# A two-layer decoder trunk on one core: input and memory rows loaded already turned, query and key heads turned by VectorE

## The reference

```
proj = rms_norm(x, a_norm) @ a_w_in      # q, k (4 heads of 96), v, o (4 heads of 192), gates (8), mq (256)
hm   = mlstm_chunkwise(q, k * 96**-0.5, v, i, f)       # f32
mo   = memory_attention(mq, *memory_kv(mem))            # 4 heads of 64 over 256 memory rows
x    = x + concat(rms_norm(hm) * sigmoid(o), mo) @ a_w_out
```

## Time and profile before

| | us |
|---|---|
| median of 3 runs (1414.15 to 1414.84) | 1414.73 |
| the profiled execution | 1414.58 |
| its span, first to last instruction | 1412.8 |
| TensorE busy | 1406.3 |
| VectorE busy | 1217.8 |
| ScalarE busy | 956.6 |
| GpSimd busy | 99.0 |

### The profile page before, as it was taken

The page is one execution under the profiler, slowest core; times in us unless marked ns, Lnnn a source line. Parts: engine busy times, 40 slices in busy tenths (PEclk is TensorE's granted clock), DMA queues, the critical chain, the costliest instruction groups (busy, mean ns, idle before and its releaser), DMA issues.

```text
span 1412.8 us, 19877 instructions
## 1 busy us (share of the span) xinstructions
PE 1406.3 (100%) x6721; PEld 1180.7 (84%) x6721; DVE 1217.8 (86%) x1186; ACT 956.6 (68%) x840; POOL 99.0 (7%) x147
## 2 busy tenths in 40 slices
PE   9999999999999999999999999999999999999999
PEld 9998888888998888888888888888888888888887
DVE  6486888878776898899999999999998999999887
ACT  7465544444685677777777777777777777777775
POOL 4020000000032020010010000001001000000000
PEclk9999999999999999999999999999999999999999
DMA  9454655554455799999999999999999999999995
GB/s 333 153 182 146 222 196 178 178 199 150 126 179 191 262 375 394 380 376 393 381 383 386 392 361 387 396 384 374 393 378 381 387 394 364 387 394 381 384 393 193
DMA packets 211824, 440.97 MB, mean 312 GB/s; under 512 B 16080, under 2 KB 56468, under 8 KB 211776
## 3 DMA queue, kind: packets, MB, share of 16 engines
q1 hardware_dynamic: 208352, 430.18, 83.3%
q0 software_dynamic: 3408, 10.16, 2.5%
q10 hardware_dynamic: 16, 0.00, 0.0%
HBM read 433.96 MB, written 6.33 MB: 312 GB/s over the span
## 4 chain that ended last, share of the span: by engine, by line
PE 98%; ACT 1%; DVE 1%; issue 0%; POOL 0%; ACTq 0%; DVEq 0%; POOLq 0%
PE PS L1731 21%; PE PS L1732 21%; PE PS L1735 21%; PE PS L1433 5%; PE PS L1434 5%; PE PS L1432 5%; PE PS L1164 3%; PE PS L1220 2%; PE PS L1212 2%; PE PS L1214 2%; PE PS L1271 1%; PE PS L1277 1%; PE PS L1274 1%; PE PS L1720 1%; PE PS L1194 1%; PE PS L1723 1%
## 5 line engine op out<-in xcount | busy, mean ns | idle before, releaser
L1886 DVE TENSOR_TENSOR wlo<-ring,whi 128x2048 fp32r<-128x2048 f32 x334 | 761.1, 2290 | 67.7 <-ACT whi L801 65.6
L801 ACT ACTIVATE whi<-ring 128x2048 fp32r<-128x2048 f32 x334 | 639.8, 1918 | 187.9 <-PE PS L1735 176.9
L1731 PE MATMUL PS<-whi,xhi 128*128 128x512 f32 x864 | 341.2, 395 | 0.0
L1732 PE MATMUL PS<-whi,xlo 128*128 128x512 f32 x864 | 336.5, 389 | 0.0
L1735 PE MATMUL PS<-wlo,xhi 128*128 128x512 f32 x864 | 231.1, 389 | 0.0
L1735 PEld LDWEIGHTS PS<-wlo,xhi 128*128 128x128 f32 x864 | 162.1, 188 | 33.9 <-DVE wlo L1886 0.3
L1731 PEld LDWEIGHTS PS<-whi,xhi 128*128 128x128 f32 x864 | 162.3, 188 | 32.7
L1732 PEld LDWEIGHTS PS<-whi,xlo 128*128 128x128 f32 x864 | 162.4, 188 | 32.2
L1731 PE MATMUL PS<-whi,hhi 128*128 128x512 f32 x440 | 171.4, 390 | 0.0
L1732 PE MATMUL PS<-whi,hlo 128*128 128x512 f32 x440 | 171.2, 389 | 0.0
L1735 PE MATMUL PS<-wlo,hhi 128*128 128x512 f32 x440 | 117.8, 390 | 0.0
(11 more groups left out here) (390 smaller groups left out, 1596.7 us busy)
## 6 DMA issues: line engine op xcount, KB each, us to landing
ring<-in_moe_w_gate_up SPq DMA_DIRECT2D x448, 512.0 KB, 6.8
ring<-in_moe_w_down SPq DMA_DIRECT2D x224, 512.0 KB, 7.1
ring<-in_dense_w_gate_up SPq DMA_DIRECT2D x56, 512.0 KB, 4.5
ring<-in_dense_w_down SPq DMA_DIRECT2D x28, 512.0 KB, 4.3
ring<-in_a_w_in SPq DMA_DIRECT2D x12, 768.0 KB, 7.7
ring<-in_mem_w_kv SPq DMA_DIRECT2D x4, 1024.0 KB, 5.5
ring<-in_a_w_out SPq DMA_DIRECT2D x4, 1024.0 KB, 5.0
ring<-in_b_w_out SPq DMA_DIRECT2D x4, 1024.0 KB, 4.9
```

Of the source, the lines that this page charges most:

```text
L801: nc.scalar.activation(whi[:, j, :], ring[:, h * SLOT:(h + 1) * SLOT], ACT.Copy).then_inc(S("highs"), 1)
L1731: mm(out_, lhsT=xh, rhs=whi[:, j, c0:c0 + HD], start=begin, stop=False)
L1732: mm(out_, lhsT=xl, rhs=whi[:, j, c0:c0 + HD], start=False, stop=False)
L1886: v.tensor_tensor(wlo[:, j, :], ring[:, h * SLOT:(h + 1) * SLOT], whi[:, j, :].bitcast(F32), ALU.subtract).then_inc(S("lows"), 1)
```

## The change

- The host hands over x and the memory rows a second time, already turned (`x_turned`, `mem_turned`: partition, block of 128, token), and all gains as one array of columns. The rows themselves are still loaded, for the squares and the residual. ScalarE's queue loads the gains and x's second pair, SyncE's the rest, in a new order among the weights.
- TensorE's transposes of x, of the memory rows, of the gains and of the q and k heads are gone. Ten warm-up matmuls stand for eight and three.
- The cuts of x and of the memory rows read SBUF. VectorE cuts the first pair of x. ScalarE's square of x moves behind items 2 and 3; its memory cuts, square("mem"), mqS and square("mq0") move behind qN. VectorE's memory low parts and norm("mem") move behind `front_lo(5)`, norm("mq0") behind the gate steps.
- VectorE turns q and k itself, in 24 transposes of 32 partitions x 256 elements (8 squares of 32x32 each), in four groups of six between the items 8 to 11. The factor 96**-0.5 moves into kN.
- GpSimd's list loses the gain transfers and nothing else.

```
-        grow = arena[0:NG, A0:A0 + P]
+        memTs = carve(5632, KD, NMEM)
+        xTs = xn[:, :, :].rearrange("p a b -> p (a b)").rearrange("p (k s) -> p k s", k=KD)
...
-            for t in range(NT):
-                sp.dma_start(xres[:, t], x_d[t * P:(t + 1) * P]).then_inc(S(f"x_in{t}"), 16)
-
+            def fill_xt(pair):
+
+                sp.dma_start(xTs[:, 2 * pair:2 * pair + 2, :], T["x_turned"][:, 2 * pair:2 * pair + 2, :]).then_inc(S(f"xt_in{pair}"), 16)
+
+            fill_xt(0)
             for part in range(2):
                 w0, view = FIRST[part], stream[0][1][:, 2 * part:2 * part + 2, :]
                 sp.dma_start(ring[:, w0].rearrange("p (k n) -> p k n", k=2), view).then_inc(S("first_in" if part == 0 else f"slot_full{place[0]}"), 16)
-            sp.wait_ge(S("x_in0"), 16)
-            for n in (1, 2):
-                fill_big(place[n], stream[n][1])
+            fill_xt(2)
+            fill_big(place[1], stream[1][1])
+            fill_xt(3)
+            fill_big(place[2], stream[2][1])
+            fill_big(place[3], stream[3][1])
+            for t in range(NT):
+                sp.dma_start(xres[:, t], x_d[t * P:(t + 1) * P]).then_inc(S(f"x_in{t}"), 16)
+            fill_big(place[4], stream[4][1])
             gb = T["a_gate_bias"].rearrange("a n -> n a")
             sp.dma_start(bias_i[:, :], gb[0:AH]).then_inc(S("bias_in"), 16)
             sp.dma_start(bias_f[:, :], gb[AH:2 * AH]).then_inc(S("bias_in"), 16)
+            fill_big(place[5], stream[5][1])
+            for half in range(2):
+                ks = slice(half * KH, (half + 1) * KH)
+                sp.dma_start(memTs[:, ks, :], T["mem_turned"][:, ks, :]).then_inc(S(f"memt_in{half}"), 16)
             for t in range(NT):
                 sp.dma_start(memS[:, t], mem_d[t * P:(t + 1) * P]).then_inc(S(f"mem_in{t}"), 16)
-            for n in (3, 4, 5):
-                fill_big(place[n], stream[n][1])
...
-            for name, v in (("b_norm", T["b_norm"][0]), ("kv_norm", T["kv_norm"]),
...
-                k = v.shape[0] // P
-                pool.dma_start(grow[gcol[name]:gcol[name] + k, :], v.rearrange("(k p) -> k p", p=P)).then_inc(S("gain_in"), 16)
...
-
...
+            def first_split_high(pair):
+
+                act.wait_ge(S(f"xt_in{pair}"), 16)
+                for k in (2 * pair, 2 * pair + 1):
+                    last = nc.scalar.activation(xhi[:, k, :], xTs[:, k, :], ACT.Copy, scale=k_gain("a_norm", k))
+                last.then_inc(S("x0_high"), 1)
+
...
-            act.dma_start(grow[0:KD, :], T["a_norm"][0].rearrange("(k p) -> k p", p=P)).then_inc(S("a_gain_in"), 16)
+            act.dma_start(gains[:, :], T["gain_columns"]).then_inc(S("gain_in"), 16)
+            act.dma_start(xTs[:, 2:4, :], T["x_turned"][:, 2:4, :]).then_inc(S("xt_in1"), 16)
             act.wait_ge(S("consts"), 3)
             nc.scalar.activation(table[:, :], ones[0:1, 0:1], ACT.Copy)
-            act.wait_ge(S("gains"), 1)
-            split_high("x0_t", "x0_high", "a_norm", 0, 0, 0)
             act.wait_ge(S("first_in"), 16)
             nc.scalar.activation(whi[:, 0, FIRST[0]], ring[:, FIRST[0]], ACT.Copy).then_inc(S("first_high"), 1)
+            act.wait_ge(S("gain_in"), 16)
+            act.wait_ge(S("x0_high"), 1)
+            first_split_high(1)
             act.wait_ge(S(f"slot_full{place[0]}"), filled_at[0])
             nc.scalar.activation(whi[:, 0, FIRST[1]], ring[:, FIRST[1]], ACT.Copy).then_inc(S("highs"), 1)
-            act.wait_ge(S("x0_high"), 2)
-            split_high("x0_t", "x0_high", "a_norm", 2, 2, 2)
+            first_split_high(2)
             front_hi(1)
-            split_high("x0_t", "x0_high", "a_norm", 3, 3, 3)
+            first_split_high(3)
+            front_hi(2)
+            front_hi(3)
             square("x0")
-            front_hi(2)
-            square("mem")
-            for b in range(4):
-                act.wait_ge(S("mem_t"), b + 1)
-                nc.scalar.activation(memhi[:, 2 * b:2 * b + 2, :].rearrange("p a s -> p (a s)"), PS[:, b, :], ACT.Copy).then_inc(S("mem_high"), 1)
-            front_hi(3)
             act.wait_ge(S("through"), through("gmq.1"))
             act.wait_ge(S("scaled"), nidx["x0"] + 1)
             for t in range(NT):
                 last = nc.scalar.activation(gS[:, t], PS[:, 4 + t, 0:2 * AH], ACT.Copy, scale=rx[:, t:t + 1])
             last.then_inc(S("gS"), 1)
             front_hi(4)
-            act.wait_ge(S("sums"), nidx["mem"] + 1)
-            for t in range(NT):
-                last = nc.scalar.activation(mqS[:, t], PS[:, 4 + t, 2 * AH:2 * AH + MW], ACT.Copy, scale=rx[:, t:t + 1])
-            last.then_inc(S("mqS"), 1)
-            act.wait_ge(S("mqS"), 1)
-            square("mq0")
             act.wait_ge(S("gate_raw"), 1)
             act.wait_ge(S("bias_in"), 32)
             nc.scalar.activation(gi, PS[0:AH, 3, 0:SEQ], ACT.Identity, bias=bias_i[:, :]).then_inc(S("gate_in"), 1)
...
             for t in range(NT):
                 last = nc.scalar.activation(qN[:, t], PS[:, 6 + t, 0:aqw], ACT.Copy, scale=rx[:, t:t + 1])
             last.then_inc(S("qN"), 1)
+            for half in range(2):
+                act.wait_ge(S(f"memt_in{half}"), 16)
+                ks = slice(half * KH, (half + 1) * KH)
+                nc.scalar.activation(memhi[:, ks, :], memTs[:, ks, :], ACT.Copy).then_inc(S("mem_high"), 1)
+            square("mem")
+            act.wait_ge(S("sums"), nidx["mem"] + 1)
+            for t in range(NT):
+                last = nc.scalar.activation(mqS[:, t], PS[:, 4 + t, 2 * AH:2 * AH + MW], ACT.Copy, scale=rx[:, t:t + 1])
+            last.then_inc(S("mqS"), 1)
+            act.wait_ge(S("mqS"), 1)
+            square("mq0")
             front_hi(6)
             act.wait_ge(S("gate_steps"), 1)
             nc.scalar.activation(gt, gt, ACT.Exp, scale=-1.0).then_inc(S("gate_in"), 1)
             act.wait_ge(S("gate_in"), 3)
             nc.scalar.activation(gt, gt, ACT.Ln, bias=1.0).then_inc(S("gate_in"), 1)
             front_hi(7)
-            act.wait_ge(S("heads_t"), 1)
-            for b in range(2):
-                last = nc.scalar.activation(qT[0:AQ, 2 * b:2 * b + 2, :], PS[0:AQ, 6 + b, :].rearrange("p (h s) -> p h s", h=2), ACT.Copy)
-            last.then_inc(S("qT"), 1)
-            act.wait_ge(S("gains"), 2)
             front_hi(8)
...
-            keep_warm(6, 8)
-            for t in range(NT):
-                pe.wait_ge(S(f"x_in{t}"), 16)
-                for pair in range(4):
-                    last = turn_pair(xres, 2 * pair, t, pair)
-                    if t == NT - 1:
-                        last.then_inc(S("x0_t"), 1)
-                if t == 0:
-                    pe.wait_ge(S("a_gain_in"), 16)
-                    tr(PS[:, 7, 0:KD], grow[0:KD, :]).then_inc(S("gains_t"), 1)
-            keep_warm(6, 3)
+            keep_warm(6, 10)
 
             project("gmq", (4, 5), xhi, xlo, "x0")
-            pe.wait_ge(S("gain_in"), 16 * 13)
-            tr(PS[:, 7, 0:NG], grow).then_inc(S("gains_t"), 1)
-            for pair in range(4):
-                for t in range(NT):
-                    pe.wait_ge(S(f"mem_in{t}"), 16)
-                    last = turn_pair(memS, 2 * pair, t, pair)
-                last.then_inc(S("mem_t"), 1)
-            pe.wait_ge(S("gains"), 2)
             project("q", (6, 7), xhi, xlo)
-            pe.wait_ge(S("mem_low"), 4)
             pe.wait_ge(S("gS"), 1)
             for g in range(2):
                 for t in range(NT):
                     last = tr(PS[0:AH, 3, g * SEQ + t * P:g * SEQ + (t + 1) * P], gS[:, t, g * AH:(g + 1) * AH])
             last.then_inc(S("gate_raw"), 1)
             project("k", (0, 1), xhi, xlo)
-            pe.wait_ge(S("qN"), 1)
-            turn_heads(qN, 6).then_inc(S("heads_t"), 1)
             pe.wait_ge(S("gate_in"), 2)
             project("v0", (2, 3), xhi, xlo)
             pe.wait_ge(S("kN"), 1)
             pe.wait_ge(S("mqS"), 1)
-            turn_heads(kN, 4).then_inc(S("heads_t"), 1)
             project("v1", (0, 1), xhi, xlo)
...
             decay_args((0, 1))
             pe.wait_ge(S("v_out"), 2)
+            pe.wait_ge(S("mem_low"), 2)
             project("memkv0", (0, 1), memhi, memlo)
...
-            dve.wait_ge(S("gains_t"), 1)
-            v.tensor_copy(gains[:, 0:KD], PS[:, 7, 0:KD]).then_inc(S("gains"), 1)
-            dve.wait_ge(S("x0_t"), 2)
-            dve.wait_ge(S("x0_high"), 1)
-            for k in (2, 3):
-                last = v.tensor_scalar(xhi[:, k, :], PS[:, 1, (k % 2) * SEQ:(k % 2 + 1) * SEQ], k_gain("a_norm", k), None, ALU.mult)
+            dve.wait_ge(S("gain_in"), 16)
+            dve.wait_ge(S("xt_in0"), 16)
+            for k in (0, 1):
+                last = v.tensor_scalar(xhi[:, k, :], xTs[:, k, :], k_gain("a_norm", k), None, ALU.mult)
             last.then_inc(S("x0_high"), 1)
-            def first_low(k):
-
```

(65 more changed lines are left out.)

22 lines of the change are left out of this document (8 added, 14 removed).

## The result

The changed kernel takes 1438.88 us (median of 4 runs, 1438.75 to 1439.63), the kernel before 1414.56 beside it (4 runs, 1414.15 to 1414.84): a ratio of 1.0173, with a 95% interval of 1.0156 to 1.0191. It is 24.3 us slower. The forecast was 1437.0, the range 1429 to 1443. The profiled execution took 1438.75, with a span of 1437.0. Of the 15 executions of the kernel before that stand beside experiments 9 to 12, one took 2343.08 us at a granted clock of 0.562 and counts in no ratio.

What follows compares the result with a forecast made beforehand. The prediction took TensorE's own list, busy 1406.3 of 1412.8 us, as the bound. It added 20.3 us for the later `decay_args` and 2 for the slow clock, 22.3 over the median of 1414.73: 1437 us, range 1429 to 1443.

Steps and rivals of the forecast that it cites:

- the wait for the masks: VectorE, ahead of front_lo(5), waits for GpSimd's masks, built behind the moved memory squares: ready at 34.9 us; called the largest step.
- rival B: Masks are not late; ScalarE's cuts, squares and mqS limit first, kT at 65.6 us: 1429 us, chance 0.1.
- end of q: At the start, q ends at 21.4 us instead of 25.5: gain 4.1 us, bounds 2.5 to 5.6.
- memory squares done: On ScalarE behind qN, two memory cuts and two squares end at 29.3 us.
- from there to the last mask: On GpSimd, 5.6 us from the end of the memory squares to the last mask, as before.
- VectorE's chain to kT: VectorE's list from the mask copies to the last transpose into kT: 38.4 us, so kT is ready at 73.3.
- `decay_args` later by: On TensorE, `decay_args` waits for kT and starts at 73.4 us instead of 53.15: a loss of 20.3 us.
- TensorE idle, three stalls: TensorE idles about 9.3 us in k.1, 5.9 in v0.1 and 11 before `decay_args`.
- slow clock behind the last stall: Matmuls in `decay_args` and memkv0 run at half rate after idling: 2 us lost, bounds 0 and 4.4.
- the price of a transpose: VectorE's 24 transposes of 32x256 turning q and k: 435 ns each, 10.4 us together, bounds 9.4 to 11.4.
- Rival C: More than one slow stretch is paid, or the memory rows land late: 1441 us, chance 0.15.
- Rival A: VectorE gets through in time and only TensorE's savings of 5.9 us show: 1408.8 us, chance 0.03.

Runs made afterwards that it cites:

- 9: Changed kernel with x's turned copy loaded by SyncE's queue in two 512 KB halves instead of four 256 KB pairs: 1437.84 us in one run.
- 10: Changed kernel with the gain columns issued on ScalarE's queue only when the first weights have landed: 1443.1 us in one run.
- 11: Changed kernel with masks first, heads on TensorE, memory squares, mqS and both norms moved later, 30 start warm-ups for ten: 1414.44 us, ratio 0.9997.
- Experiment 12: Changed kernel with 30 warm-up matmuls at the start instead of 10: 1437.04 us, ratio 1.0161.
- 1: Changed kernel with GpSimd's masks built ahead of rstd_of("x0") and rstd_of("mem"): 1432.09 us, ratio 1.0127.
- 2: Changed kernel with the q and k heads turned by TensorE again and masks still late: 1427.74 us, ratio 1.0092.
- 3: Changed kernel with both edits, masks built first and heads turned by TensorE: 1421.92 us, ratio 1.0052.
- 6: Kernel before with only the heads turned by VectorE (24 transposes) and the factor of kN changed: 1425.05 us, ratio 1.0074.
- Experiment 5: Masks first, heads on TensorE, memory work moved behind front_hi(7) on ScalarE and front_lo(8) on VectorE, norm("mq0") spanning front_lo(9), against the changed kernel: 1420.91 us.
- 8: Changed kernel with x's second turned pair loaded by SyncE's queue behind the first, not by ScalarE's: 1439.69 us, ratio 1.0175.
- experiment 4: Changed kernel with 80 warm-up matmuls on TensorE ahead of `decay_args`: 1436.01 us, ratio 1.015.

## Why the prediction was right, step by step

**The two causes and the path were right.** The masks wait behind the memory squares, VectorE waits for the masks with everything behind it, and the transposes lengthen its list; the end is kT. Experiments 1 and 2 take each cause away alone, 3 both, and 6 shows the second by itself in the kernel before. The parts overlap: 6.8 for the masks, 11.1 for the heads, 17.0 for both. The prediction calls the wait for the masks the largest step. It is the longest idle time of VectorE, but taken away it gives back less than the transposes, because ScalarE's block stands right behind it as the next limit. The prediction's list held a third part that it named only under rival B, the memory block and norm("mq0") ahead of `front_lo(7)`. Experiment 5 missed because moving them about ahead of kT doesn't take them off the path; in 11, with both norms behind kT, the squares behind the copy of qT and the start kept warm, the loss is gone.

**The sizes**, each term beside what it measured:

| step | predicted | measured |
|---|---|---|
| end of q (before 25.50) | 21.4 | 23.97 |
| memory squares done | 29.3 | 31.7 |
| from there to the last mask | 5.6 | 4.2 |
| last mask | 34.9 | 35.9 |
| VectorE's chain to kT | 38.4 | 38.75 |
| `decay_args` later by | 20.3 | 21.6 |
| TensorE idle, three stalls | 9.3, 5.9, 11 | 7.5, 3.5, 9.8 |
| slow clock behind the last stall | 2 | 24.3 - 21.6 = 2.7 |

**The start was mis-sized: "Gain 4.1 us" was 1.5**, below its own lower bound of 2.5; in the other six profiles with this start q ends 1.6 us earlier to 0.1 later than before. Two things failed. The byte sums took the rates of before for the new order, 238 and 401 GB/s in the second and third slices, and the new transfers got 105 and 194, so the first weights landed at about 6.6 instead of 4.9 and the first matmul came at 7.32 instead of 5.5. And ten warm-ups end at 4.86, so TensorE stands for 2.47 us and gmq runs at half rate until about 12.5; the prediction charged the clock behind the late stalls and forgot the one at the start. Experiment 12 gives that part a price, 1.24 us at the end of q in this pair of profiles and 1 to 3 over all of them. The low rate itself isn't explained: neither one queue (8), nor larger pieces (9), nor later gains (10) restore it, and a different combination wasn't tried.

**The masks came 1.0 us late instead of 2.4**, because the second error has the other sign: 5.6 us from the squares to the last mask held a select of 2.05 us, and it took 0.63 here. VectorE was subtracting at that time before, and stands still now. That the second error takes 1.4 us back from the first is luck.

**The chain was right to 0.4 us**, and the price of a transpose was the one taken from the rows: 24 at a mean of 435 ns, started some 447 ns apart. The Trainium skill, "VectorE: DVE Perf Modes", section "The three transpose paths", has 311 ns for a 128x128 bf16 tile, and an estimate from that figure makes the wait 6.7 us shorter. The page gives no figure for this form, and by these traces that of bf16 doesn't carry over to float32 transposes of 32x256. Experiment 6 shows the cost of the whole in the time.

**The idle times are each 1.2 to 2.4 us shorter than foretold, though `decay_args` is later.** TensorE came into every stall later than assumed, by the 2.6 us of the start and by the slow stretches behind the first two stalls (2.93 us for the eight matmuls at 39.07). Those hide behind VectorE, as said. Of the stalls behind q only the last has a slow stretch that is paid: experiment 4 returns 2.9 us, and in 2 and 6 the difference between time and `decay_args` is 2.6. Rival C asked for more than one that is paid. There was a second, but at the start, where C didn't look for it, and it stands in the lost gain. The memory rows weren't late (ScalarE squares the second block with no wait). Rival A is excluded by the 12.74 us, rival B by the same line.

The sum came out 1.9 us low. The squares were 2.4 us late, the way to the last mask 1.4 shorter, the chain 0.4 longer and the clock 0.7 dearer: 2.4 - 1.4 + 0.4 + 0.7 = 2.1, the rest is rounding and the 0.17 us between the two medians of the kernel before. That it came so near rests in part on luck, the late start against the shorter way to the last mask. The chain and the price of the clock don't.

## What to carry to other kernels

An edit that takes work off the bounding engine is paid by the engines that feed it: before counting the saving, write the feeder's list with its durations from the trace and see where its last entry ends. Here an earlier start of 1.5 us and 1.8 us of TensorE's transposes were exchanged for 10.4 us on VectorE, which had 7.4 to spare, and for a block moved on ScalarE on which GpSimd, and through one wait VectorE, depended. When a block moves on one engine, look for every list that waits for its result and for what stands behind that wait, even where the two have nothing to do with each other, as the masks and the memory rows.
